# Second block's mixer: new order of the gates, the SiLUs and the exponentials on ScalarE, closing norms squared on ScalarE

## The reference

```python
def gated_deltanet(q, k, v, z, b, a, conv_w, a_log, dt_bias, norm_g):
    qkv = jax.nn.silu(causal_depthwise_conv(concat([q, k, v]), conv_w))
    ...
    beta = sigmoid(b)
    g = -exp(a_log) * softplus(a + dt_bias)
    G = cumsum(g);  q, k = l2norm(q), l2norm(k)
    ... # decays exp(G_i - G_j), a triangular solve, a state over two chunks
    o = rmsnorm(o, norm_g) * silu(z)

def hgrn2(q, f, i, g, lb, norm_g):
    ... # gates from sigmoid(f), a state over four chunks
    o = rmsnorm(o, norm_g) * silu(g)

def rmsnorm(x, g):
    return x * lax.rsqrt(mean(x * x) + 1e-6) * g

mix = concatenate([o_a, o_b, o_c]) @ w_out      # deltanet, sparse attention, hgrn2
```

## Time and profile before

| | us |
|---|---|
| median of three runs | 4314.92 (4314.73 to 4317.37) |
| the profiled execution | 4316.6 |
| its span in the trace | 4314.8 |

### The profile page before, as it was taken

How to read it: one execution, slowest core, us unless ns; L and a number is a source line. 1 busy time by engine, 2 the same in 40 slices (tenths; PEclk the granted TensorE clock), 3 DMA queues, 4 the chain that set the end, 5 groups by cost and what they waited for, 6 DMA issues and landing times. The chain is left out here.

```text
span 4314.8 us, 66458 instructions
## 1 busy us (share of the span) xinstructions
PE 3970.2 (92%) x25922; PEld 3546.9 (82%) x25922; DVE 3058.7 (71%) x6865; ACT 1832.6 (42%) x2893; POOL 5.8 (0%) x16
## 2 busy tenths in 40 slices
PE   7997999999999999999989899999997887978698
PEld 5766999988879989888868799998886777878597
DVE  3556797778876867788854678777887666656674
ACT  3343444433343444434342444443334525554363
POOL 0000000000000000000000000000000000000000
PEclk8998999999999999999979999999998998989899
DMA  5142565556666855567621356556665213442143
GB/s 205 71 173 101 174 211 180 171 192 241 243 239 236 320 200 166 182 238 254 244 104 62 130 199 216 173 166 211 247 240 190 107 54 123 164 148 87 60 157 122
DMA packets 122677, 755.32 MB, mean 175 GB/s; under 512 B 15808, under 2 KB 17344, under 8 KB 57984
## 3 DMA queue, kind: packets, MB, share of 16 engines
q1 hardware_dynamic: 122368, 751.08, 49.6%
HBM read 695.45 MB, written 55.57 MB: 174 GB/s over the span
## 5 line engine op out<-in xcount | busy, mean ns | idle before, releaser
L1847 DVE TENSOR_TENSOR expert_ring_low<-expert_ring,expert_high 128x1024 fp32r<-128x1024 f32 x768 | 935.1, 1219 | 265.6 <-ACT expert_high L2060 265.2
L2060 ACT ACTIVATE expert_high<-expert_ring 128x1024 fp32r<-128x1024 f32 x768 | 811.2, 1057 | 654.4 <-PE ps L2011 653.6
L1979 PE MATMUL ps<-peer_hT_high_peer,expert_high 128*128 128x256 f32 x3072 | 886.6, 289 | 10.0 <-DVE expert_ring_low L1847 9.7
L1980 PE MATMUL ps<-peer_hT_low,expert_high 128*128 128x256 f32 x3072 | 865.2, 282 | 0.0
L1981 PE MATMUL ps<-peer_hT_high_peer,expert_ring_low 128*128 128x256 f32 x3072 | 864.9, 282 | 0.0
L1979 PEld LDWEIGHTS ps<-peer_hT_high_peer,expert_high 128*128 128x128 f32 x3072 | 587.8, 191 | 12.6 <-DVE expert_ring_low L1847 11.8
L1980 PEld LDWEIGHTS ps<-peer_hT_low,expert_high 128*128 128x128 f32 x3072 | 588.5, 192 | 0.0
L1981 PEld LDWEIGHTS ps<-peer_hT_high_peer,expert_ring_low 128*128 128x128 f32 x3072 | 583.2, 190 | 0.0
L2011 PE MATMUL ps<-expert_high,weighted_high 128*128 128x512 f32 x1536 | 476.1, 391 | 27.3 <-DVE weighted_low L1874 27.3
L2011 PE MATMUL ps<-expert_ring_low,weighted_high 128*128 128x512 f32 x1536 | 475.4, 391 | 0.0
L2011 PE MATMUL ps<-expert_high,weighted_low 128*128 128x512 f32 x1536 | 474.5, 390 | 0.0
(11 more groups left out here) (630 smaller groups left out, 7126.2 us busy)
## 6 DMA issues: line engine op xcount, KB each, us to landing
expert_ring<-in_peer_u SPq DMA_DIRECT2D x192, 1024.0 KB, 5.3
expert_ring<-in_peer_v SPq DMA_DIRECT2D x192, 1024.0 KB, 4.9
gelu_peer<-gelu_out SPq DMA_DIRECT2D x192, 256.0 KB, 5.5
gelu_in_peer<-gelu_peer SPq DMA_DIRECT2D x96, 512.0 KB, 5.7
weight_ring<-in_ffn_w_up SPq DMA_DIRECT2D x22, 2048.0 KB, 7.3
weight_ring<-in_w_in SPq DMA_DIRECT2D x14, 2048.0 KB, 7.3
weight_ring<-in_w_mod SPq DMA_DIRECT2D x12, 2048.0 KB, 7.4
weight_ring<-in_peer_wq SPq DMA_DIRECT2D x12, 2048.0 KB, 7.3
```

Source lines behind the costliest of these rows:

```text
L1847: dve.tensor_tensor(piece(low, n), piece(raw, n), high[:, n % LEAD, :].bitcast(F32), ALU.subtract).then_inc(low_done, 1)
L1979: pe.matmul(o, b[:, s], hT_h[:, c, :], start=(c == 0), stop=False)
L1980: pe.matmul(o, b[:, s], hT_l[:, c, :], start=False, stop=False)
L2060: act.activation(high[:, n % LEAD, :], piece(raw, n), ACT.Identity).then_inc(high_done, 1)
```

## The change

1. Gates: beta no longer comes from ScalarE's sigmoid but from exp(-b) on ScalarE and an addition and a reciprocal on VectorE. exp(a_log) goes to the front of the stage, right after the first group's convolution tap. exp(-b), exp and ln of the softplus now stand on ScalarE's list before the second half of the squares, and `hg_g`'s SiLU after the root. VectorE's additions for g and TensorE's two small matmuls come earlier. VectorE's order is now: copies to `dn_nat`, beta, the epsilon of the squares, g, the reciprocal of the root, and L3021 (now L3026) in two halves with the cumulative sums between them. Before, g stood between the reciprocal and L3021.
2. The third group's SiLUs come one after the other, and one pair of decays moves ahead of them.
3. The last SiLU of z is put ahead of the exponential L3624.
4. Closing norms: squares and sums straight from PSUM on ScalarE (four activations with an accumulator per half), the scale and epsilon in the root's own scale and bias; the multiplication by the root's inverse reads PSUM. The copies, squares, sums and scalings on VectorE go.
5. The norms' weights are multiplied into the two SiLU tiles early (new `gains`, four multiplications on VectorE amid the attention), so that one multiplication a tile goes at the end.

```diff
-    GATES = 46.0
+    GATES = 42.2
+    SILU = (4.8, 4.8, 5.7)
@@ conv_tap0
-                yield at + 4.8 + 0.4 * (n % 4)
+                yield at + self.SILU[g] + (0.4 if g < 2 else 0.01) * (n % 4)
@@ gates_act
-        yield T
-        act.wait_ge(S.consts_landed, B.consts)
+        yield 21.8
         act.activation(B.ea[:, :], B.row[:, 0, :], ACT.Exp).then_inc(S.act_step, 1)
+        yield T + 0.3
         for job in self.small_jobs:
             act.wait_ge(*self.in2.evicted(job))
-        act.activation(B.ba[:, :, :], B.small[:, :, 64:68], ACT.Sigmoid).then_inc(S.act_step, 1)
-        yield T + 0.6
+        act.activation(B.ba[:, :, :], B.small[:, :, 64:68], ACT.Exp, scale=-1.0).then_inc(S.act_step, 1)
...
-        yield T + 2.8
+        yield T + 7.0
...
-        yield T + 5.2
+        yield T + 9.5
@@ gates_pe
-        yield self.GATES + 4.0
+        yield self.GATES + 5.5
@@ gates
-        yield T + 2.0
+        yield T + 2.2
+        dve.wait_ge(S.act_step, 2)
+        step(dve.tensor_scalar(B.ba[:, :, :], B.ba[:, :, :], 1.0, None, ALU.add))
+        step.wait()
+        dve.reciprocal(B.ba[:, :, :], B.ba[:, :, :]).then_inc(S.beta_ready, 1)
+        yield T + 4.4
@@ decays
-        S, B, step, T = self.S, self.B, self.step, self.GATES + 6.6
+        S, B, step, T = self.S, self.B, self.step, self.GATES + 10.6
@@ out_act
-        yield T + 5.0
-        act.wait_ge(S.dn_ms_ready, 1)
-        act.activation(B.dn_ms[:, 0, :, 1], B.dn_ms[:, 0, :, 0], ACT.Sqrt).then_inc(S.dn_rms_ready, 1)
...
+        for t in range(2):
+            yield T + (2.4, 7.2)[t]
+            act.wait_ge(*((S.first_ready, 1), (S.second_ready, 1))[t])
+            for h in range(4):
+                last = act.activation(B.sq[:, t, h, :], self.bank((4, 7)[t])[:, h, :], ACT.Square, accum_out=B.dn_ms[:, t, h, 0:1])
+            last.then_inc(S.dn_ms_ready, 1)
+            act.wait_ge(S.dn_ms_ready, t + 1)
+            act.activation(B.dn_ms[:, t, :, 1], B.dn_ms[:, t, :, 0], ACT.Sqrt, scale=1.0 / DN_DHEAD,
+                           bias=B.eps[:, 0:1]).then_inc(S.dn_rms_ready, 1)
+
+    def gains(self, dve):
+        S, B = self.S, self.B
+        yield 117.0
+        dve.wait_ge(S.s_out, self.in2.total["s"])
+        dve.wait_ge(S.norms_landed, 32)
+        for t in range(2):
+            dve.tensor_tensor(B.sz[:, t, :], B.sz[:, t, :], B.wdn[:, :], ALU.mult).then_inc(S.gained, 1)
+            yield 118.5 + 3 * t
+            dve.tensor_tensor(B.cg[:, t, :], B.cg[:, t, :], B.whg[:, :], ALU.mult).then_inc(S.gained, 1)
+            yield 120.0
@@ out (out_norm is gone)
+        for t in range(2):
+            yield T + (4.6, 9.4)[t]
+            dst = B.cat[:, t, 0:512].rearrange("p (h c) -> p h c", h=4)
+            dve.wait_ge(S.dn_rms_ready, t + 1)
+            step(dve.reciprocal(B.dn_ms[:, t, :, 0], B.dn_ms[:, t, :, 1]))
+            step.wait()
+            step(dve.tensor_tensor(dst, self.bank((4, 7)[t]), B.dn_ms[:, t, :, 0:1].broadcast_to([P, 4, P]), ALU.mult))
+            step.wait()
+            dve.wait_ge(S.gained, 4)
+            step(dve.tensor_tensor(dst, dst, B.sz[:, t, :].rearrange("p (h c) -> p h c", h=4), ALU.mult))
@@ Hgrn.after_act
-        yield self.TURN + 4.4
+        yield self.TURN + 5.4
```

107 lines of the change are left out of this document (31 added, 76 removed).

## The result

The changed kernel takes 4269.3 us (median of 4 runs, 4258.48 to 4272.93); the kernel before 4314.82 us (4 runs, 4306.11 to 4317.37). The ratio is 0.9894, with a 95% interval of 0.9871 to 0.9917: faster by 45.5 us. Predicted were 4273.0 us, range 4266 to 4286.

A forecast was written before the change was run, and what follows sets the result against it. TensorE bounds both stages, by its waits for normalised q and k, last SiLU and weighted values, and a stage end on VectorE. Terms of -22.0 and -19.8 us, -41.8 from the 4314.92 us median, give 4273 us, range 4266 to 4286.

The forecast's parts named there:

- First SiLUs: Start of the stage: early exponential of a_log and its load delay the first transposes, +0.85 us a pass, bounds 0 and 1.5.
- Gates: Normalised q and k: root right behind the squares lets transposes start earlier, -7.7 us a pass, bounds -6.7 and -7.9.
- Clock behind the gates: TensorE after the gates: idle time now some 2 us, so less clock lost, -0.5 us a pass, bounds 0 and -0.9.
- Weighted values: Third group: three table loads become two, VectorE's 0.90 us wait goes, -0.9 us a pass, bounds -0.5 and -1.3.
- Last SiLU: Attention: TensorE's wait for `silu_z` goes, with the half clock behind it, -6.6 us first pass, -4.4 second.
- Early weights: Attention: the norms' weight multiplications on VectorE delay its next output, +0.4 us a pass, bounds 0 and +1.1.
- End of the stage: After TensorE's last matmul: 3.3 us to the last multiplication instead of 10.75, -7.5 us a pass, bounds -6.3 and -8.5.
- the second rival: Gates keep part of their wait: ScalarE reaches the last squares late, root late by 3.2 us; 4282 us, chance 0.07.
- the dear bound of twice that: End of the stage: if each square from PSUM took twice 0.3 us, 1.2 us of the gain goes.
- the clock's: Rival: new short gaps at first SiLUs and gates bring half clock, 3.9 us a pass lost; 4281 us, chance 0.13.
- The rival of the weights' DMA: Attention: VectorE waits for the norms' weights landing late, so the kernel is slower; 4324 us, chance 0.01.
- 4262 us: Estimate for the whole kernel if each of four loads fewer a pass were worth 1.38 us more, 11 us in all.

The follow-up runs named there:

- the gates alone: Kernel before with only the plan of the gates changed (root ahead of gates, beta by exponential and reciprocal, early exp(a_log), third group's SiLUs together): 0.9961 of before.
- the later `gains`: Changed kernel with one closing multiplication beside the root and the second pair of `gains` multiplications some 6 us later: 0.9892 of the kernel before.
- the squares on VectorE: Changed kernel with copy, square and sum for the delta rule's two halves on VectorE again: 0.9917 of the kernel before.
- the gates filled: Changed kernel with TensorE's two waits at the gates filled by 8 and 12 throwaway transposes: 0.9884 of the kernel before, 4255.52 us.
- the last SiLU alone: Kernel before with only the last SiLU put ahead of the exponential: 0.9979 of before.
- three fills with two small edits: Changed kernel, three TensorE waits filled with transposes, exp(a_log) back among beta's exponentials, one closing multiplication beside the root, second `gains` pair later: 4254.49 us, 0.9865 of before.

## Why the prediction was right

Each term as the two traces have it, from the same points in both (us, first / second pass; the columns of "measured" add up to the stages' -24.15 and -21.97 with 0.02 of rounding):

| term | predicted | measured |
|---|---|---|
| first projection piece, no term | 0 | -1.11 / +0.06 |
| First SiLUs | +0.85 | +0.67 / +0.78 |
| Gates (start of the transposes, counted from the end of the jobs behind the first SiLUs) | -7.7 | -7.66 / -7.78 |
| Clock behind the gates (to the start of the second job behind them) | -0.5 | +0.52 / -0.29 |
| Weighted values (on to the end of the last projection piece) | -0.9 | -2.62 / -3.10 |
| Last SiLU, with Early weights | -6.2 / -4.0 | -6.44 / -4.14 |
| End of the stage | -7.5 | -7.51 / -7.50 |
| outside the mixer, no term | 0 | +2.5 in all |

- **First SiLUs.** Right in kind and within the bounds. TensorE's new wait at L2921 is 0.46 and 0.57 us; the run with the gates alone puts the cost at 0.66 and 0.67 us, and the one that takes the early load out gets 0.66 and 0.79 back.
- **Gates.** The size is right, one step of its working holds only in some passes. "The last four squares still wait for VectorE's copy" failed in this profile: ScalarE came to the squares at 3374.57 us behind the ln, the copy had ended at 3374.20. This is the second rival's mechanism, but at 0.4 us, not 3.2. It cost nothing against the forecast because the copy was itself 1.95 us earlier from the stage's start than the rows of before had it, most of it by the job ahead of it, which ran at full clock (3.08 us, not 4.60). Where that job took 4.6 us again (the gates alone and the later `gains`, first pass; the squares on VectorE, both), the copy ended last and the root's load stood 1.33 us behind it, as forecast. The transposes start 11.50 to 11.56 us behind the jobs either way. And in this profile the wait did not become one of "some 2 us" but two, 1.29 us for g and 2.13 us for the norm: the sums of g stand behind the addition to `dn_ms` on VectorE.
- **Clock behind the gates.** The step that failed: "the idle time is now some 2 us", from which I took a better clock. The job behind the gates took 4.93 us where it took 4.02 behind ten idle us, and 5.06 where it took 4.95. Two waits of 1.3 and 2.1 us cost as much clock here as one of 10 us; the run that filled them got 2.2 and 2.4 us back.
- **Weighted values.** Undersized. I priced only the 0.90 us wait of the earlier trace rows. VectorE had two more waits for ScalarE in that stretch, of 0.66 and 0.40 us for pieces of weights, and all three are gone: 1.96 us. On top, job 11 behind the shorter wait runs at full clock in the changed kernel, 3.11 us where it took 4.13 and 4.64. "The 3.6 us wait does not go" was half right: it is 1.84 us in the profile where job 9 ahead of it runs at half clock, and 3.29 us where it does not. The count of loads was off too: not three of the third group's became two but four became two, each 1.28 us on the ScalarE that VectorE waited for.
- **Last SiLU.** Right in both passes. Alone it is worth 6.85 and 4.52 us, 0.2 us more than said, and the split in the first pass holds: with the wait kept and the clock restored 2.83 us came back, where the term had 2.5. The exponential got a wait of its own for the product, 1.32 us, as said.
- **Early weights.** 0.35 us in both passes, at L3455, and it is `gains`: moved later, the wait is gone.
- **End of the stage.** 3.79 us instead of 11.30 in both passes. The squares from PSUM took 0.28 us, inside the assumption of 0.3, so the dear bound of twice that did not come. The rule to give multiplications to VectorE (the Trainium skill, ScalarE: Activation LUTs, Rules for kernel authors) was weighed with numbers that were right in sign; the run with the squares on VectorE says what following it costs here, 4.3 and 3.9 us.
- **Outside the mixer.** No term. From the stage's end to the next pass's first projection matmul it took 268.92 us after 267.99, and from the second stage's end to the end of the program 261.2 after 259.8. The sum left out the next stage's clock, or rather held 1 us of gain there possible: its first long run of products (L559) took 24.41 and 24.64 us where it took 23.88 and 23.89, and 24.43 and 24.62 when the changed kernel was profiled again. That is 1.3 of the 2.3 us. That the shorter gap ahead of it is the cause isn't shown: behind the same gap of 3.79 us it took 23.85 and 24.12 us with the gates filled, and behind the old gap of 11.30 us 24.61 us in the second pass of the last SiLU alone. This and the other 1.0 us stay open.

Of the rivals, the clock's came true in part: it does fall behind gaps of 1.3 us, and it took 0.5 us in the first pass behind the gates, but not behind the new 0.46 us at the first SiLUs, where the job behind the next wait even ran at full clock in both passes of this profile (with the same two waits it took 4.6 us in four passes of other runs). The Trainium skill, TensorE: Matmul & The Clock Gate, section HAM oscillation, has it that only gaps above a certain length bring the clock down, which would forbid such a fall behind one or two us; the table of jobs contradicts it: job 5 took 4.93 and 5.06 us behind waits of 1.29 and 2.13 us, and 3.12 us with them filled. The rival of the weights' DMA did not occur: no wait for it stands at `gains`. The table loads cost 1.28 us with the next activation following within 0.02 us, so 4262 us, worked out from the 2.66 us of the Trainium skill, ScalarE: Activation LUTs, section What ACT_TABLE_LOAD costs, was the wrong price.

The sum was right partly by luck, by errors that cancel: the clock behind the gates and the time outside the mixer were put 1.2 and 2.5 us too low (both passes), the weighted values 3.9 us (both passes) too small, and one projection piece gave 1.1 us that is no one's. That the absolute time fell into the range is luck too: five later runs of the changed kernel have a median of 4262.73 us, below the 4266, beside 4307.41 us for the kernel before, and only the ratio stayed (0.9898; the forecast of 41.8 us is 0.9903). A slip without consequence: the bounds at their dear end add up to -28.6 us, not -27, which gives 4286 and is the range's own end.

## What to carry to other kernels

Price a wait at its length only if the engine's clock is whole behind it, and fill a wait of TensorE that can't be removed with throwaway transposes into a bank about to be overwritten: here three fills with two small edits beat an already faster kernel by 10.6 us in its two stages and 8 us in the medians. Before crediting a gain, ask whether the stretch stands ahead of a wait (then it is worth nothing) or behind it (then all of it), and when an engine's list runs without idle to the end of a stage, take operations off that list, whoever does them instead. Compare kernels by stages counted from a point inside the trace when whole runs scatter by more than the edit is worth.

## What the runs showed of the hardware that I had not expected

**Half clock without any idle time.** The changed kernel was profiled twice. The two executions differ by 10.2 us of span, and nearly all of it lies in one stretch of 30 us far ahead of the mixer, in code no edit touched. Ten us of it in the first profile:

```profile
2225.00:2235.00 10.00, 10.00 (x28) 6.12 (x28) 1.92 (x2) 4.89 (x9) 0.00 (x0) 0.50 0.00 0
```

and in the second:

```profile
2222.00:2232.00 10.00, 10.00 (x47) 5.72 (x45) 3.07 (x4) 6.61 (x11) 0.00 (x0) 1.00 0.00 0
```

In both windows TensorE is busy all 10.00 us, at 0.50 in the one and 1.00 in the other. Nor does a gap stand ahead of the first: TensorE had been busy without one since 2206.93 us, at 1.00 from 2215 to 2220 us, when the clock fell. So idle time is what costs the clock inside the mixer, as the fills show, but it is not the only thing that does, and what decides here is open. The mixer's first matmul lies at 3332.0 to 3335.1 us in 6 of the 12 other profiles and at 3322.7 to 3325.1 us in 6; the kernel before had 3334.44 us in the profile on which the prediction rests. Its median over the 31 runs beside the first experiments is 4306.68 us, 8 us below the 4314.92 us of the three runs shown at first. Ratios are not moved by this, since both kernels are measured side by side, but an absolute time from three runs can be.

**The fall depends on more than the gap.** The same 0.70 us wait for the second SiLUs is followed by a job of 4.60, 4.11, 3.08 and 3.09 us in the two kernels' passes; the 2.13 us wait at the gates, where none of 1.3 us stands ahead of it, by 4.16 to 4.26 us in four passes and by 3.12 in one; and the same 1.34 us left by the fillers by a clock of 1.00 in one pass and 0.71 in the other. A fall costs a 3.1 us job 0.6 to 2.2 us.

**Squares from PSUM.** A square with a sum of 128x128 from PSUM took 279 ns (mean of 8) against 298 ns from SBUF, and of 128x64 220 ns; PSUM as a source costs no more. The root with scale and a bias from a tile took 298 ns where the plain one took 208 ns.
